# Experts: gates for eight keys in 1 KB runs, V picks that end three steps sooner, norms of the gathered tiles beside the last right-half blocks

## The reference

```python
def block(xb):                      # idx, g: 8 x 16 picks of a token and their gates
    u = expert_u[idx]
    h = gelu(einsum('thkd,td->thk', u, xb), approximate=False)
    w = g * h
    return einsum('thk,thkd->td', w, expert_v[idx])
...
x = layer_norm(ALPHA * x + ffn, ln2_g, ln2_b)
```

## Time and profile before

| | |
|---|---|
| median of three runs | 2846.3 us |
| profiled execution | 2848.69 us, its span 2846.6 us |
| PE busy | 2617.2 us (92%) |
| VectorE busy | 2258.7 us (79%) |
| ScalarE busy | 919.1 us (32%) |
| GpSimd busy | 1314.0 us (46%) |
| first matmul of the expert phase | 1153.10 us |
| gate loads | 32, of 1280 KB |

### The profile page before, as it was taken

How to read it: one execution, slowest core, us unless ns; L and a number is a source line. 1 busy time by engine, 2 the same in 40 slices (tenths; PEclk the granted TensorE clock), 3 DMA queues, 4 the chain that set the end, 5 groups by cost and what they waited for, 6 DMA issues and landing times.

```text
span 2846.6 us, 47358 instructions
## 1 busy us (share of the span) xinstructions
PE 2617.2 (92%) x17459; PEld 1711.9 (60%) x17459; DVE 2258.7 (79%) x4533; ACT 919.1 (32%) x1603; POOL 1314.0 (46%) x869
## 2 busy tenths in 40 slices
PE   7999888999867755899999999999999999999996
PEld 3566655669867744565565565665665665665653
DVE  4244454657999998788988988898989988989998
ACT  2333333531125545432232232232322322322324
POOL 2110011010034442356767756676677666657672
PEclk9999997999979865899999999999999999999998
DMA  4000202430002244999999999999999999999995
GB/s 161 23 16 16 74 9 96 146 122 1 2 31 118 118 184 185 327 378 365 345 330 364 369 360 346 350 350 337 346 362 363 334 355 352 343 342 370 333 344 220
DMA packets 274011, 682.16 MB, mean 240 GB/s; under 512 B 29448, under 2 KB 111880, under 8 KB 269456
## 3 DMA queue, kind: packets, MB, share of 16 engines
q0 software_dynamic: 110592, 402.70, 38.0%
q1 hardware_dynamic: 163216, 276.73, 27.3%
HBM read 622.73 MB, written 56.62 MB: 239 GB/s over the span
## 4 chain that ended last, share of the span: by engine, by line
PE 43%; DMA 6%; issue 5%; DVE 3%; POOL 1%; ACT 1%; DVEq 0%; ACTq 0%; SPq 0%; POOLq 0%
PE h_psum L1976 22%; PE o_psum L1987 21%; DMA early<-u_blocks 4%; DVE wide L1829 2%; DMA early<-v_blocks,pick_index 1%; POOL early L1540 1%; DMA early<-v_blocks 0%; DVE wide L1817 0%; DVE wide L1928 0%; DMA fetched<-v_blocks,pick_index 0%; DVE early L1795 0%; DVE act_out L1782 0%; DVE v_split L1802 0%; ACT v_split L1697 0%; ACT w_split L1706 0%
## 5 line engine op out<-in xcount | busy, mean ns | idle before, releaser
L1976 PE MATMUL h_psum<-early 128*128 128x384 bf16 (+1 forms) x6144 | 857.7, 300 | 7.5 <-DVE early L1795 4.6
L1987 PE MATMUL o_psum<-v_split,w_split 128*128 128x512 bf16 x3840 | 849.7, 379 | 2.9 <-DVE v_split L1802 1.7
L1976 PEld LDWEIGHTS h_psum<-early 128*128 128x128 bf16 x6144 | 601.6, 98 | 263.4 <-issue 11.1
L1987 PEld LDWEIGHTS o_psum<-v_split,w_split 128*128 128x128 bf16 x3840 | 375.6, 98 | 436.3 <-DVE v_split L1802 2.1
L1540 POOL DMA_INDIRECT early<-u_rows,pick_index x320 | 450.9, 1409 | 261.8 <-DVE dots L1825 184.8
L1540 POOL DMA_INDIRECT early<-v_blocks,pick_index x320 | 462.6, 1445 | 218.8 <-DVE wide L1829 138.4
L1829 DVE SCALAR_TENSOR_TENSOR wide<-early,dots,wide 128x1024 f32<-128x1024 f32 x320 | 405.6, 1279 | 24.8 <-DMA early<-v_blocks,pick_index 23.0
L1825 DVE CUSTOM_DVE_ANT_0 early<-early,wide 128x1024 f32<-128x1024 f32 x320 | 386.1, 1217 | 16.6 <-DMA early<-u_rows,pick_index 15.8
L1697 ACT ACTIVATE v_split<-early 128x512 bf16<-128x512 f32 x256 | 159.4, 623 | 326.4 <-PE o_psum L1987 253.7
L1689 ACT ACTIVATE act_out<-h_psum 128x384 f32<-128x384 f32 (+1 forms) x256 | 97.7, 433 | 443.1 <-PE h_psum L1976 420.7
L1101 PE MATMUL r_t_psum<-x_t,early 128*128 128x128 f32 (+1 forms) x1920 | 234.7, 284 | 0.0
(11 more groups left out here) (215 smaller groups left out, 2924.7 us busy)
## 6 DMA issues: line engine op xcount, KB each, us to landing
early<-u_blocks SPq DMA_DIRECT2D x128, 512.0 KB
early<-v_blocks SPq DMA_DIRECT2D x256, 256.0 KB
gates<-wide SPq DMA_DIRECT2D x20, 2048.0 KB, 6.4
gate<-gates SPq DMA_DIRECT2D x32, 1280.0 KB
early<-w_query SPq DMA_DIRECT2D x8, 1024.0 KB, 5.8
early<-w_fox SPq DMA_DIRECT2D x4, 1536.0 KB, 7.1
early<-u_rows,pick_index POOLq DMA_INDIRECT x320
early<-v_blocks,pick_index POOLq DMA_INDIRECT x320
```

Of the source, the lines that this page charges most:

```text
L1976: mm = pe.matmul(h_psum[:, half, 0:width * P], u_split[:, q % 2, part, c], xs[:, first:first + width, xpart, c, :], start=(c == 0 and part ...
L1987: mm = pe.matmul(o_psum[t][:, :], w_split[:, w_slot(r, q), part, t * P:(t + 1) * P], v_split[:, k, vpart], start=(q == 0 and part + vpart ...
```

## The change

The gate tile holds two groups of eight keys (`GATE_KEYS`) in place of two groups of four, so that a run of one partition and chunk is 1 KB in place of 512 B. A load brings half of the chunks of a group and has the size of a load before, 1280 KB, and two loads fill a group. At the start both loads of the first group are issued ahead of the U block of key 2. The LayerNorm parameters have no tiles of their own; they are loaded into the two U buffers at the end, in the step q = 15 of the last period. The V takes end three half-two steps earlier. In the last half two, ScalarE does the moments of the three gathered tiles in steps 9, 10 and 11 (behind the high halves of V blocks 12, 13 and 14) and VectorE their norms in steps 10, 11 and 12 (behind the low halves of V blocks 13, 14 and 15), and the dense tiles alone are left behind the last matmul. The order of the additions between the norms is moved accordingly. Two hunks that only replace `ln_g[:, :]` by `ln_g` and `ln_b[:, :]` by `ln_b` are left out.

```diff
@@ -1512,6 +1512,7 @@
 AHEAD = 2
 HALF = D_MODEL // 2
 V_RING = 4
+GATE_KEYS = SPAN // 2
 
 
 def early_xs(early):
@@ -1560,7 +1561,8 @@
     WEIGH_STEP = SPAN - 2
     U_END = WEIGHED * PERIOD_SHARE - 3 * Y_SHARE
     V_START = WEIGHED * PERIOD_SHARE - 2 * Y_SHARE
-    V_END = PERIODS * PERIOD_SHARE - 6 * Y_SHARE
+    V_END = PERIODS * PERIOD_SHARE - 9 * Y_SHARE
+    NORM_FROM = 2 * SPAN - 7
     LAST = PERIODS - 1
     TOGETHER = V_RING
     with ExitStack() as ctx:
@@ -1573,11 +1575,10 @@
         u_split = (early[:, EARLY:EARLY + 2 * KD * P].bitcast(BF16)
                    .rearrange("p (k h c n) -> p k h c n", k=2, h=2, c=KD))
         v_split = sb("v_split", [P, V_RING, 2, HALF], BF16)
-        gate = sb("gate", [P, 2, TOKENS // CHUNK, GROUP, CHUNK], F32)
+        gate = sb("gate", [P, 2, TOKENS // CHUNK, GATE_KEYS, CHUNK], F32)
         act_out = sb("act_out", [P, 2, TOKENS], F32)
         w_split = sb("w_split", [P, SPAN + 1, 2, TOKENS], BF16)
-        ln_g = sb("ln2_g_sb", [P, D_MODEL], F32)
-        ln_b = sb("ln2_b_sb", [P, D_MODEL], F32)
+        ln_g, ln_b = u_raw[:, 0], u_raw[:, 1]
 
         beyond = sb("fetched", [P, RING - EARLY_ROWS, D_MODEL], F32)
         fetched = early_rows(early) + [beyond[:, r] for r in range(RING - EARLY_ROWS)]
@@ -1623,8 +1624,9 @@
                     i, m = i + m // (2 * SPAN), m % (2 * SPAN)
                     load_v_half(sp, v_raw, v_blocks, v_in, SPAN * i + m % SPAN, m // SPAN, m % V_RING)
 
-                def load_gate(i, g):
-                    sp.dma_start(gate[:, g % 2], gates[:, :, bass.ds(SPAN * i + g * GROUP, GROUP), :]
+                def load_gate(i, g, part):
+                    some = slice(part * TOKENS // CHUNK // 2, (part + 1) * TOKENS // CHUNK // 2)
+                    sp.dma_start(gate[:, g % 2, some], gates[:, some, bass.ds(SPAN * i + g * GATE_KEYS, GATE_KEYS), :]
                                  ).then_inc(gate_in[g % 2], 16)
 
                 def refill(i, r=0, first=False, end=False):
@@ -1635,16 +1637,21 @@
                             load_u(i, q + AHEAD + 3)
                         sp.wait_ge(v_lo_done, 2 * SPAN * i + q + V_RING)
                         load_v(i, q + 2 * V_RING - 1)
-                        done = q + AHEAD
-                        if done % GROUP == 0 and not (end and done // GROUP + 2 > SPAN // GROUP):
+                        done, part = q + AHEAD, (q + AHEAD) % GATE_KEYS // 4
+                        if first and done in (AHEAD + 1, AHEAD + 3):
+                            load_gate(0, 1, done // 2 - 1)
+                        if done % 4 == 0 and done >= GATE_KEYS and not end:
                             sp.wait_ge(gated, SPAN * i + done)
-                            load_gate(i, done // GROUP + 1)
+                            load_gate(i, done // GATE_KEYS + 1, part)
+                        if done == 4 and not first:
+                            sp.wait_ge(gated, SPAN * i + done)
+                            load_gate(i, 1, 1)
                         if first and q % 2 == 1 and q // 2 < DENSE:
                             load_rows_of_x1(sp, GATHERED + q // 2, GATHERED + q // 2 + 1)
-                        if first and q == 2 * DENSE + 1:
-                            sp.dma_start(ln_g[:, :], ln2_g.partition_broadcast(P)).then_inc(ln_in, 16)
-                        if first and q == 2 * DENSE + 3:
-                            sp.dma_start(ln_b[:, :], ln2_b.partition_broadcast(P)).then_inc(ln_in, 16)
+                        if end and q == SPAN - 1:
+                            sp.wait_ge(u_lo_done, N_KEYS)
+                            sp.dma_start(ln_g, ln2_g.partition_broadcast(P)).then_inc(ln_in, 16)
+                            sp.dma_start(ln_b, ln2_b.partition_broadcast(P)).then_inc(ln_in, 16)
                     for q in range(SPAN, 2 * SPAN):
                         if not (end and q + 2 * V_RING - 1 >= 2 * SPAN):
                             sp.wait_ge(v_lo_done, 2 * SPAN * i + q + V_RING)
@@ -1652,7 +1659,8 @@
 
                 for k in range(2):
                     sp.wait_ge(stage_stored[k], n_stored)
-                load_gate(0, 0)
+                load_gate(0, 0, 0)
+                load_gate(0, 0, 1)
                 for q in range(2):
                     sp.wait_ge(u_lo_done, q + 1)
                     load_u(0, q + 2)
@@ -1660,7 +1668,6 @@
                 for m in range(V_RING - 1):
                     sp.wait_ge(v_lo_done, m + 1)
                     load_v(0, m + V_RING)
-                load_gate(0, 1)
                 sp.wait_ge(u_lo_done, AHEAD + 1)
                 load_u(0, AHEAD + 2)
                 refill(0, first=True)
@@ -1751,7 +1758,9 @@
                             act.activation(dots_all[:, :, :], dots_all[:, :, :], ACT.Gelu).then_inc(dots_gelu, 1)
                         if q < SPAN and b < N_KEYS:
                             gelu(b)
-                for t in range(TILES):
+                        if i == LAST and 0 <= q - NORM_FROM < GATHERED:
+                            moments(q - NORM_FROM)
+                for t in range(GATHERED, TILES):
                     moments(t)
 
             @block.gpsimd
@@ -1774,10 +1783,10 @@
                 dve.memset(eps[:, :], LN_EPS).then_inc(eps_set, 1)
 
                 def gate_block(b):
-                    g, q = b // GROUP, b % GROUP
+                    g, q = b // GATE_KEYS, b % GATE_KEYS
                     dve.wait_ge(gelu_done, b + 1)
                     if q == 0:
-                        dve.wait_ge(gate_in[g % 2], 16 * (g // 2 + 1))
+                        dve.wait_ge(gate_in[g % 2], 32 * (g // 2 + 1))
                     rows = act_out[:, b % 2].rearrange("p (c t) -> p c t", t=CHUNK)
                     dve.tensor_tensor(rows, rows, gate[:, g % 2, :, q, :], ALU.mult).then_inc(gated, 1)
 
@@ -1933,15 +1942,19 @@
                     if t == 0:
                         dve.wait_ge(ln_in, 32)
                         dve.wait_ge(row_used, TAKES)
-                    while added[0] < min(t - 1, DENSE):
-                        add(2 * PERIODS - 1, added[0])
-                        added[0] += 1
-                    if t > 0:
+                    if t == GATHERED:
+                        root(t - 1)
+                        finish(t - 1)
+                    if t >= GATHERED:
+                        while added[0] < min(t - GATHERED + 2, DENSE):
+                            add(2 * PERIODS - 1, added[0])
+                            added[0] += 1
+                    if t > 0 and t != GATHERED:
                         root(t - 1)
                     if t < TILES:
                         dve.wait_ge(squared, t + 1)
                         scale_rows(t)
-                    if t > 0:
+                    if t > 0 and t != GATHERED:
                         finish(t - 1)
 
                 taken, added = [0], [0]
@@ -1957,7 +1970,9 @@
                         half_one_step(i, q)
                     for q in range(SPAN):
                         half_two_step(i, q)
-                for t in range(TILES + 1):
+                        if i == LAST and 0 < SPAN + q - NORM_FROM <= GATHERED:
+                            norm(SPAN + q - NORM_FROM - 1)
+                for t in range(GATHERED, TILES + 1):
                     norm(t)
 
             @block.tensor
```

More of the change, by code:

```diff
@@ L1909, in scale_rows @@
                     dve.wait_ge(mean_made, t + 1)
-                    dve.scalar_tensor_tensor(acc[:, t], acc[:, t], neg_mean[:, t:t + 1], ln_g[:, :], ALU.add, ALU.mult
+                    dve.scalar_tensor_tensor(acc[:, t], acc[:, t], neg_mean[:, t:t + 1], ln_g, ALU.add, ALU.mult
                                              ).then_inc(scaled, 1)
@@ L1927, in finish @@
                     dve.wait_ge(rstd_step, 4 * t + 4)
-                    dve.scalar_tensor_tensor(acc[:, t], acc[:, t], rstd[:, t:t + 1], ln_b[:, :], ALU.mult, ALU.add
+                    dve.scalar_tensor_tensor(acc[:, t], acc[:, t], rstd[:, t:t + 1], ln_b, ALU.mult, ALU.add
                                              ).then_inc(rows_done, 1)
```

## The result

The changed kernel takes 2850.85 us (median of 20 runs, 2846.9 to 2853.08) beside 2846.59 us for the kernel before (20 runs, 2840.46 to 2851.65). The ratio of these runs is 1.0014 with a 95% interval of 1.0008 to 1.0021, so 4.0 us (2.3 to 6.0) slower; the two medians differ by 4.3. The profiled execution lasted 2850.61 us with a span of 2848.5 us, which is 1.9 us more than the 2846.6 of before; the two profiles show the mechanisms, and less of the cost than the medians.

A forecast was written before the change was run, and what follows sets the result against it. PE's unbroken stream was taken to bound the kernel, leaving only start and tail to move the time. +2.9 (U block) + 2.0 (clock) - 2.6 (end) + 0 (middle) = +2.3 us gave 2848.6, range 2842.8 to 2852.0.

The forecast's parts named there:

- PE's stream: Middle, the eight periods: PE runs almost unbroken, so the change there brings 0, with -1 to +2 us.
- the rival that the takes open some: Middle: late VectorE makes PE wait for the gelu, 5 us at one in ten steps, 2853.6 us; chance 0.10.
- The gates ahead of the U block: Start: two gate loads ahead of key 2's U block delay PE's third product by 2.9 us (1.9 to 4.2).
- the free start: Start: the U block isn't held up, sharing the engines with the gates; -2.6 us, 2843.7 us; chance 0.17.
- The clock: Start: PE's 3.9 us of idleness lowers its granted clock, costing 2.0 us (0 to 2.3).
- The long-gates rival: Start: 1 KB runs pass at the 512 B rate, so the start costs 4.2 + 2.0; 2849.9 us; chance 0.13.
- The parameter loads: Last half-two part: the two broadcasts delay the last takes by none to 2.6 us; end taken at 2802.
- The last stop: Ahead of the last 60 matmuls: gathered moments hold V block 15, so PE idles 3.9 us instead of 1.67.
- The tail: Behind the stream: fewer norms remain, last finish 3.2 us earlier, less 0.6 for the clock: 2.6 us gain.
- full end: End: the norms don't hold the last block, gain 7.3 us; chance 0.08 (2843.9 or, with undelayed start, 2839.0).

The follow-up runs named there:

- picks_only: The kernel before with V_END three half-two steps earlier, nothing else changed: 2846.61 us, ratio 0.9999.
- two_loads_512: The kernel before with its second gate load (four keys, 512 B runs) moved ahead of the U block of key 2: 2853.90 us, ratio 1.0025.
- last_in_order: The changed kernel with ScalarE's third gathered moments behind V block 15 and VectorE's norms 1 and 2 after its low half: 2851.21 us.
- start_by_keys: The changed kernel with the first gate group loaded as keys 0 to 3 ahead of the U block, 4 to 7 behind the V blocks: 2845.09 us.
- late_parameters: The changed kernel with the LayerNorm parameter loads behind the last V block, not ahead of V block 7: 2850.36 us, ratio 1.0014.
- norms_only: The changed kernel with the gate tile, its loads and waits as in the kernel before: 2845.01 us, ratio 0.9993.
- gates_only: The changed kernel with V picks and norms put back as in the kernel before; parameters stay in the U buffers: 2852.85 us, ratio 1.0020.
- adds_first: start_by_keys with ScalarE's third moments behind V block 15 and VectorE's first two dense additions between the gathered norms: 2843.42 us, ratio 0.9987.

## Why the prediction was right, and where it was off

The time was forecast as 2848.6 with 2842.8 to 2852.0 and no difference beyond 0.2%; it is 2850.85, 0.14% slower. It lies inside that range, but 0.85 us above the forecast's own range of 2846.5 to 2850. The sum of +2.3 us is at the lower edge of what was measured (2.3 to 6.0). The kind of every term was right; the delay of the U block was taken too small, the clock's price and the gain of the end too large.

*PE's stream.* Right. In none of the kernels does anything between the third product and the last 180 matmuls set the time; the stretch takes 1593.2 us in each profile but that of before. That profile has 1.3 us more, 1.0 of them in two waits for the gelu at 2555.66 and 2685.91. picks_only and two_loads_512, both with the gate layout of before and the latter with its takes too, need 1593.2, so the waits seem to belong to that one execution and are no gain of the change. No gaps opened, so the rival that the takes open some is out.

*The gates ahead of the U block.* Right in place and kind, small in size. 2.9 us were forecast; the four profiles with this start show 3.11, 3.17, 3.76 and 4.30 us more idleness, 3.6 on average. The U block comes 3.4 to 4.2 us later, counted from SP's issue, where 3.1 were forecast. The rate explains a part at most: it is 323 to 336 GB/s over the window that holds the slow microsecond, but 361 to 368 behind it in these profiles, which is about the 356 that I interpolated. Why the block comes another 0.3 to 1.1 us later isn't shown. That it came later at all rules out the free start.

*The clock.* Right that it falls, 2.0 us forecast, 1.3 to 1.7 measured in these four profiles and 2.3 behind the longer stop of two_loads_512. Together the start was to cost 4.9 us; the profile of the change has 4.8, the other three 4.8, 5.4 and 5.6 (of the 5.6, last_in_order, 0.6 are only its faster first product, 8.35 us in place of 8.96), and the medians of the change and of start_by_keys differ by 5.8.

*The long-gates rival and the page behind it.* It fell on its premise. The Trainium skill, "DMA: Bandwidth & Descriptors", section Specifications, has line rate from 512 B on; here 512 B runs passed at 294 to 301 GB/s, 1 KB runs at 323 to 336 with the slow microsecond and 361 to 368 behind it, 4 KB at 408. The measurement decides: the rate still grows well beyond 512 B. But what the runs gain, 0.8 to 1.5 us for two loads, is less than the second load costs by standing ahead. The time that this rival gave, 2849.9, is nearer to the measured one than mine; it owes that to the start's cost being larger, not to the rate.

*The parameter loads.* The term "none to 2.6 us of delay of the takes, I take 2802" was mis-sized a little. The last take ended at 2806.8, which with the 3.9 us by which PE's 180 matmuls start later is 2802.9. late_parameters shows 1.3 us of delay.

*The last stop.* ScalarE's queue holds the last block, with VectorE's close behind, as written: 3.9 us forecast, 3.67 without the late rows, 4.95 with them. In the changed kernel the table load took 1.28 us (2809.66), the first root started at 2810.96 and the split of block 13 at 2811.16. The drain of about 1.38 us that the Trainium skill, "ScalarE: Activation LUTs", section What ACT_TABLE_LOAD costs, adds isn't seen here either.

*The tail.* 2.6 us of gain forecast, 2.0 measured (1.6 in norms_only and start_by_keys). From the first dense addition to the last finish the walk has 19.8 us, and the change took 19.65 (2824.53 to 2844.18), so this stretch was right; what was short is the stop before it, taken at 3.9 us and measured at 4.95. But the step that priced the "full end" at 7.3 us failed. I walked VectorE's queue from the first dense tile and left out that with PE's stop unchanged the norms of the gathered tiles stand behind block 15 in that same queue. last_in_order shows 31.46 - 28.90 = 2.6 us, and even with additions in front and rows in time the gain is 31.46 - 26.24 = 5.2.

*What the parts of the sum add up to.* +5.8 (start) - 1.8 (the rest) = +4.0 us by the medians, in place of +4.9 - 2.6. Each of the two was off by less than 1 us, both to the same side, so no error hid another. That the clock fell wasn't luck either: behind all nine stops of 3.67 us and more in the table it did.

## What to carry to other kernels

In a stream that runs without a gap, the transfers that cost time here were those ahead of its start and those beside its last blocks, and none between. Count what each DMA in the issuing queue puts ahead of the block that the first wait needs, and make a load bigger only behind it. Work moved beside the last blocks must not stand ahead of them in any queue, the one that splits them included. A stop that is removed brings only what the next queue lets through: write out the engine that ends last, from the last block on, before pricing the gain.

## What the runs showed of the hardware

The rate by run length, in this mix of SP's loads: 512 B 298 to 301 GB/s over the windows with the slow microsecond and 294 behind it, 1 KB 323 to 336 and 361 to 368, 4 KB 408. In steady flow the profile's DMA share is 1.21 with 512 B runs, 1.06 with 1 KB and 1.02 with 4 KB.

The clock didn't follow the length of the stop alone. Behind last stops of 1.67, 2.07 and 2.85 us the 60 matmuls took 13.11 us, full speed; behind 2.38, 3.67, 4.95, 5.11 and 5.17 us they took 14.8 to 15.7. The granted clock says the same: 1.00 from 2818 to 2822 in gates_only (2.85 us), 0.50 from 2813 to 2815 in adds_first (2.38 us). So 2.38 us cost 1.7 us more and 2.85 us nothing, though PE had been busy at a clock of 1.00 for hundreds of microseconds ahead of both. A short stop has two prices, and which of them it gets can't be read from its length.
